# The first half-step's down projection as seven block products, with their differences and weight sums on Pool

## What is computed

```python
def swiglu(h, wg, wu, wd):
    return (jax.nn.silu(h @ wg) * (h @ wu)) @ wd

def ffn_half(x, g, wg, wu, wd):
    return x + 0.5 * swiglu(rms_norm(x, g), wg, wu, wd)
...
        x = ffn_half(x, g_ffn1[l], w1_gate[l], w1_up[l], w1_down[l])
        u = rms_norm(x, g_mix[l])
        qkv, z, qm, gates = split_proj(u, w_in[l])
```

## Time and profile before

| | |
|---|---|
| median of three timed runs | 2451.17 us |
| profiled execution, span from first to last instruction | 2449.4 us |
| gate and up stage of the first half-step, PE's first matmul to its last | 35.7 to about 506 us |
| down projection, PE's first matmul to its last | 506.5 to 755.1 us |
| busy PE, DVE, ACT, Pool over the span | 97%, 58%, 38%, 25% |

### The profile page before, as it was taken

One profiled execution on the slowest core, in us unless ns is written; L12 is line 12 of the kernel. 1 busy time (PEld: TensorE's weight loads), 2 busy tenths in 40 slices (PEclk: granted clock), 3 DMA queues, 4 the chain that ended last, 5 costly groups with the idle time before them and its releaser, 6 DMA issues.

```text
span 2449.4 us, 41688 instructions
## 1 busy us (share of the span) xinstructions
PE 2371.0 (97%) x16883; PEld 2321.8 (95%) x16883; DVE 1420.3 (58%) x2364; ACT 920.4 (38%) x1906; POOL 614.8 (25%) x614
## 2 busy tenths in 40 slices
PE   5899999999999999999899999999699999999998
PEld 4899999999998899999899999999699999999998
DVE  7766666645565274544364644468866566654546
ACT  5433343334453132333332222145433333333544
POOL 1544444501120020000200200014445444431100
PEclk7999999999999999999999999999999999999999
DMA  3122222265553461122342633124122222255645
GB/s 108 53 79 79 78 79 87 70 208 183 185 186 117 157 209 42 58 64 63 84 141 81 188 98 130 44 78 129 57 83 79 79 78 79 79 173 170 201 161 176
DMA packets 176934, 275.10 MB, mean 112 GB/s; under 512 B 11461, under 2 KB 124613, under 8 KB 176360
## 3 DMA queue, kind: packets, MB, share of 16 engines
q1 hardware_dynamic: 159848, 208.75, 26.3%
q0 software_dynamic: 16896, 63.70, 7.9%
HBM read 227.57 MB, written 44.84 MB: 111 GB/s over the span
## 4 chain that ended last, share of the span: by engine, by line
PE 46%; DVE 2%; ACT 1%; issue 1%; DMA 0%; POOL 0%; SPq 0%; DVEq 0%; ACTq 0%
PE ps L426 9%; PE ps L427 9%; PE ps L428 9%; PE ps L1162 6%; PE ps L1163 6%; PE ps L1164 6%; DMA blend_late_l<-mem_out 0%; PE ps L2889 0%; PE ps L927 0%; DVE ul_full L533 0%; DVE ul L2685 0%; DVE ul L529 0%; DVE blend_rights L529 0%; ACT uh L525 0%; DVE ffn_tok L960 0%
## 5 line engine op out<-in xcount | busy, mean ns | idle before, releaser
L426 PE MATMUL ps<-uh,stream_high 128*128 128x352 f32 (+1 forms) x1392 | 457.7, 329 | 8.6 <-DVEq L2727 7.0
L427 PE MATMUL ps<-uh,stream_low 128*128 128x352 f32 (+1 forms) x1392 | 446.5, 321 | 0.0
L428 PE MATMUL ps<-ul,stream_high 128*128 128x352 f32 (+1 forms) x1392 | 444.7, 319 | 0.0
L426 PEld LDWEIGHTS ps<-uh,stream_high 128*128 128x128 f32 x1392 | 262.8, 189 | 19.7 <-issue 16.9
L1277 DVE TENSOR_TENSOR ffn_part<-ffn_part,ps 128x258 f32<-128x258 f32 x352 | 147.1, 418 | 210.9 <-PE ps L1164 148.9
L427 PEld LDWEIGHTS ps<-uh,stream_low 128*128 128x128 f32 x1392 | 262.8, 189 | 1.6 <-issue 1.0
L428 PEld LDWEIGHTS ps<-ul,stream_high 128*128 128x128 f32 x1392 | 262.8, 189 | 0.0
L1196 ACT ACTIVATE ffn_part<-ps 128x258 f32<-128x258 f32 x264 | 102.0, 386 | 423.3 <-PE ps L1164 415.4
L1162 PE MATMUL ps<-uh,ffn_lefts_h 128*128 128x258 f32 x704 | 199.1, 283 | 6.3 <-ACT ffn_part L1196 3.4
L1162 PE MATMUL ps<-uh,stream_high 128*128 128x258 f32 x704 | 199.6, 284 | 3.2 <-ACT ffn_part L1196 3.2
L1163 PE MATMUL ps<-uh,ffn_lefts_l 128*128 128x258 f32 x704 | 199.0, 283 | 0.0
(11 more groups left out here) (374 smaller groups left out, 6273.6 us busy)
## 6 DMA issues: line engine op xcount, KB each, us to landing
ffn_raw_d<-in_w_down SPq DMA_DIRECT2D x66, 512.0 KB, 3.3
stream_raw<-in_w_in SPq DMA_DIRECT2D x25, 1024.0 KB, 5.5
ffn_hid_out<-ffn_hid SPq DMA_DIRECT2D x88, 258.0 KB, 2.4
stream_raw<-in_w_gate SPq DMA_DIRECT2D x22, 1024.0 KB, 5.3
stream_raw<-in_w_up SPq DMA_DIRECT2D x22, 1024.0 KB, 5.6
stream_raw<-in_w_down SPq DMA_DIRECT2D x88, 256.0 KB, 3.1
stream_raw<-in_w_out SPq DMA_DIRECT2D x22, 512.0 KB, 3.9
ffn_raw_d<-in_w_down SPq DMA_DIRECT2D x44, 256.0 KB, 3.1
```

The costliest lines, as they stand in the source:

```text
L426: pe.matmul(out, w_high, a_high, start=first, stop=False)
L427: pe.matmul(out, w_low, a_high, start=False, stop=False)
L428: return pe.matmul(out, w_high, a_low, start=False, stop=last)
```

## The change

The down projection's product is cut into two by two blocks on each side: output halves of 512 channels, hidden tiles by pairs (the even and the odd tile of a pair), and columns in two blocks (n = 0, 1) of twice 258. Seven products of such blocks, each over all 11 pairs, replace the eight.

- **Operands.** `Pieces` prepares them during the gate and up stage. For each pair Pool makes the four weight sums (`Pieces.gpsimd`) and, for each j, the four differences of hidden blocks in three instructions (`differ`), and SP stores rows, differences and sums to memory. They are formed in the space of `x`, which is stored once after the first side and comes back in four pieces (`load_x`).
- **Rounds.** `Rounds` runs the products one after another in the order of `ROUNDS`, 7 rounds of 11 steps. A step loads 128x512 of weights or sums and 2x258 columns into a ring of six, where the raw data and the low part share their space; the load of step s therefore waits until step s - 6 is done. Each step is 2 x 4 banks x 3 matmuls of 258 columns. `OPENS` names the rounds that clear the banks; the others go on accumulating. Behind the split of step 3 of a round DVE adds the previous round's banks onto one block of `x` (`INTO`).
- **Seam.** The last four steps run first for j = 0 and then for j = 1. Squares and split parts are made in rounds 4 to 6 and during those last steps; what concerns the last quarter (`LATE`) is done in the next stage, whose third unit now begins with four mean matmuls and whose DVE list begins with four reciprocals of 258 columns.

The diff, cut to its core:

```diff
-class Down:
...
+ROUNDS = (5, 3, 2, 1, 6, 7, 4)
+OPENS = (5, 2, 1)
+INTO = {5: (1, 1), 3: (0, 1), 2: (0, 0), 1: (0, 0), 6: (0, 1), 7: (1, 1), 4: (1, 0)}
...
+    def load(self, sp, p, rights):
+        if p == 0:
+            sp.wait_ge(self.x_stored, 16)
+            sp.wait_ge(rights.gained, 4)
+            sp.wait_ge(rights.gained_act, 4 * K2)
+        else:
+            sp.wait_ge(self.summed, 4 * p)
+        sp.dma_start(self.raw, self.w[:, 2 * p:2 * p + 2, :]).then_inc(self.down_in, 16)
...
+    def store_sums(self, sp, p):
+        sp.wait_ge(self.summed, 4 * (p + 1))
+        sp.dma_start(self.cols[:, :, p, :], self.sums).then_inc(self.sums_stored, 16)
...
+    def gpsimd(self, gp, p):
+        low, high = (slice(half * WIDE, (half + 1) * WIDE) for half in range(2))
+        gp.wait_ge(self.down_in, 16 * (p + 1))
+        if p:
+            gp.wait_ge(self.sums_stored, 16 * p)
+        gp.tensor_tensor(self.sums[:, 0, :], self.raw[:, 0, high], self.raw[:, 1, high], ALU.add).then_inc(self.summed, 1)
+        gp.tensor_tensor(self.sums[:, 2, :], self.raw[:, 0, low], self.raw[:, 0, high], ALU.subtract
+                         ).then_inc(self.summed, 1)
+        gp.wait_ge(self.summed, 4 * p + 1)
+        gp.tensor_tensor(self.sums[:, 1, :], self.sums[:, 0, :], self.raw[:, 0, low], ALU.subtract
+                         ).then_inc(self.summed, 1)
+        gp.wait_ge(self.summed, 4 * p + 3)
+        gp.tensor_tensor(self.sums[:, 3, :], self.raw[:, 1, low], self.sums[:, 1, :], ALU.subtract
+                         ).then_inc(self.summed, 1)
...
+    def differ(self, gp, p, j, hid, hid_ready, rights):
+
+        at = 3 * (2 * p + j)
+        d = self.diffs
+        gp.wait_ge(*hid_ready)
+        if p == 0:
+            gp.wait_ge(self.x_stored, 16)
+            gp.wait_ge(rights.gained, 4)
+            gp.wait_ge(rights.gained_act, 4 * K2)
+        else:
+            gp.wait_ge(self.diffs_stored[j], 16 * p)
+        gp.tensor_tensor(d[:, j, 0:2, :], hid[:, j, 1:4:2, :], hid[:, j, 0:2, :], ALU.subtract).then_inc(self.differed, 1)
+        gp.wait_ge(self.differed, at + 1)
+        gp.tensor_tensor(d[:, j, 2, :], hid[:, j, 3, :], d[:, j, 0, :], ALU.subtract).then_inc(self.differed, 1)
+        gp.wait_ge(self.differed, at + 2)
+        gp.tensor_tensor(d[:, j, 3, :], hid[:, j, 2, :], d[:, j, 2, :], ALU.subtract).then_inc(self.differed, 1)
...
+    RING = 6
+    STEPS = len(ROUNDS) * PAIRS
+    GROUPS = 2 * HO
+    APART = 4
+    LEAD = 4
+    PIECE_AT = 5
+    X_AT = (None, 14, 20, 44)
...
+    def load(self, sp, s):
+        r, p = divmod(s, PAIRS)
+        product_of, slot, pieces = ROUNDS[r], s % self.RING, self.pieces
+        if s >= self.RING:
+            self.wait_step(sp, s - self.RING)
+        if product_of in DIRECT:
+            tile, half = DIRECT[product_of]
+            src = pieces.w[:, 2 * p + tile, half * WIDE:(half + 1) * WIDE]
+        else:
+            sp.wait_ge(pieces.sums_stored, 16 * (p + 1))
+            src = pieces.cols[:, SUM_SLOT[product_of], p, :]
+        sp.dma_start(self.left_raw[:, slot, :], src).then_inc(self.left_in[slot], 16)
+        for stored in pieces.rows_stored if ROW_SLOT[product_of] < 4 else pieces.diffs_stored:
+            sp.wait_ge(stored, 16 * (p + 1))
+        sp.dma_start(self.right_raw[:, slot, :, :], pieces.rows[:, ROW_SLOT[product_of], p, :, :]
+                     ).then_inc(self.right_in[slot], 16)
...
+        half, block = self.X_ORDER[n]
+        for j in range(2):
+            at = slice(half * HO, (half + 1) * HO)
+            sp.dma_start(self.m.x[:, at, columns(block, j)], self.pieces.x_out[:, at, columns(block, j)]
+                         ).then_inc(self.x_back[n], 16)
+
+    def sync(self, sp):
+        for s in range(self.RING, self.STEPS):
+            if s in self.X_AT:
+                self.load_x(sp, self.X_AT.index(s))
+            self.load(sp, s)
...
+    def tensor(self, pe, s, js, taken):
+        r, p = divmod(s, PAIRS)
+        slot, opens = s % self.RING, ROUNDS[r] in OPENS
+        pe.wait_ge(self.ready, s + 1)
+        for j in js:
+            for i in range(HO):
+                b = HO * j + i
+                if p == 0 and r == 0 and i == 0:
+                    pe.wait_ge(taken, TAKES * (2 * SIDES - 1 + j))
+                if p == 0 and r:
+                    pe.wait_ge(self.added, self.GROUPS * (r - 1) + b + 1)
...
+                pe.matmul(out, w_h, a_h, start=opens and p == 0, stop=False, skip_group_check=True)
+                pe.matmul(out, w_l, a_h, start=False, stop=False, skip_group_check=True)
+                last = pe.matmul(out, w_h, a_l, start=False, stop=p == PAIRS - 1, skip_group_check=True)
+                if p == PAIRS - 1:
+                    last.then_inc(self.done, 1)
+        if p < PAIRS - 1 and len(js) == 2:
+            last.then_inc(self.step_done, 1)
...
+        for s in range(together):
+            self.tensor(pe, s, (0, 1), taken)
+        for j in range(2):
+            for s in range(together, self.STEPS):
+                self.tensor(pe, s, (j,), taken)
...
+        slot, count = s % self.RING, 16 * (s // self.RING + 1)
+        act.wait_ge(self.left_in[slot], count)
+        act.activation(self.left_h[:, slot, :], self.left_raw[:, slot, :], ACT.Copy).then_inc(self.rounded, 1)
+        act.wait_ge(self.right_in[slot], count)
+        act.activation(self.right_h[:, slot, :, :], self.right_raw[:, slot, :, :], ACT.Copy).then_inc(self.rounded, 1)
...
+    def add(self, dve, r, j, i):
+        half, block = INTO[ROUNDS[r]]
+        b = HO * j + i
+        if b == 0:
+            dve.wait_ge(self.x_back[self.X_ORDER.index((half, block))], 32)
+        dve.wait_ge(self.done, self.GROUPS * r + b + 1)
+        x = self.x_piece(half * HO + i, block, j)
+        dve.scalar_tensor_tensor(x, self.m.ps[:, b, 0:QW], 0.5, x, ALU.mult, ALU.add).then_inc(self.added, 1)
...
+    def tensor(self, pe, c):
+
+        u, self.unit = self.unit, self.unit + 1
+        before = len(self.WHOLE + self.FIRST)
+        if u == 0:
+            pe.wait_ge(self.low, before)
+        if u == 1:
+            pe.wait_ge(self.low, before + HO)
+        if u == 2:
+            pe.wait_ge(self.summed, before - 2)
...
+                pe.matmul(self.m.ps[:, self.BANKS[b], 0:QW], self.m.mean[:, :], self.m.rstd[:, columns(n, j)],
+                          start=True, stop=True).then_inc(self.meaned, 1)
+        if u == 3:
+            pe.wait_ge(self.rooted, 4)
...
+    def vector(self, dve):
+        for i, (o, n, js) in enumerate(self.LATE):
+            self.low_of(dve, len(self.WHOLE + self.FIRST) + i + 1, o, n, js)
+        dve.wait_ge(self.summed, len(self.WHOLE + self.FIRST) - 2)
...
+            late = self.m.rstd[:, columns(0, 1)]
+            dve.tensor_tensor(late, late, self.late_sq[:, i, :], ALU.add).then_inc(self.late_summed, 1)
...
                     lefts.load(sp, q + 1)
+                    if pieces and q == 0:
+                        pieces.store_x(sp)
+                    if pieces and q and q % 2 == 0:
+                        pieces.store_diffs(sp, q // 2 - 1, 1)
+                        pieces.store_sums(sp, q // 2 - 1)
+                    if pieces and q % 2:
+                        pieces.load(sp, q // 2, rights)
                 elif then is not None:
                     sp.wait_ge(lefts.ready, ALL * SIDES)
                     stream.load(sp, stream.base, *then)
                 if finish and q == SIDES - 1:
                     finish.sync_first(sp, (lefts.ready, ALL * SIDES))
+                if pieces and q == SIDES - 1:
+                    pieces.load(sp, q // 2, rights)
                 if q % 2:
                     store(q // 2, 0)
+                    if pieces:
+                        pieces.store_diffs(sp, q // 2, 0)
                     if q == SIDES - 1:
                         if finish:
                             finish.sync_second(sp, (product_done, done(q, 0, ALL - 1)))
                         else:
                             sp.wait_ge(product_done, done(q, 0, ALL - 1))
-                            for s in range(DOWN_RING):
+                            for s in range(down.RING):
                                 down.load(sp, s)
                     store(q // 2, 1)
             if finish:
                 finish.sync(sp)
                 return
-            for s in range(DOWN_RING, DOWN_STEPS):
-                down.load(sp, s)
+            pieces.store_sums(sp, PAIRS - 1)
+            pieces.store_diffs(sp, PAIRS - 1, 1)
+            down.load_x(sp, 0)
+            down.sync(sp)
 
         @block.tensor
         def _(pe):
...
+            for s in range(3, down.STEPS):
+                r, p = divmod(s, PAIRS)
                 down.vector(dve, s)
...
+                if r and p == down.LEAD - 1:
+                    for j in range(2):
+                        for i in range(HO):
+                            down.add(dve, r - 1, j, i)
```

(74 more changed lines are left out.)

241 lines of the change are left out of this document (155 added, 86 removed).

## The result

The changed kernel took 2463.45 us (median of 4 runs, 2461.56 to 2464.86) against 2451.18; the ratio is 1.0048, 95% interval 1.0034 to 1.0062. The forecast was 2433.5, its range 2421 to 2447. In a later series of nine runs the same kernel took 2458.17, ratio 1.0025 [1.0016, 1.0035].

A forecast was written before the change was run, and what follows sets the result against it. TensorE's matmuls were taken to bound both the gate and up stage and the down projection. Terms: -27.6 + 0.5 + 4.2 + 3.1 + 2.6 - 0.5 = -17.7 us, from 2451.17 to 2433.5 us; range 2421 to 2447.

The forecast's parts named there:

- Pool in the gate and up stage: Gate and up stage: Pool's added sums and differences fit where it waits; cost 0.5 us for the whole stage, from 0 to 10.
- The fourth rival: Gate and up stage: VectorE and Pool hold each other up, 0.5 us in each of 20 sides; 2443, chance 0.08.
- The rival on the slower side: Gate and up stage: Pool becomes the bound, 44 us a pair against 40.2, 42 us more, 2475; chance 0.08.
- Matmuls: Down projection: 1848 matmuls of 258 columns take 221.0 us against 248.6 before, -27.6 us.
- Step 6: Down projection, first round: TensorE waits 4.2 us, from 0 to 8, for a load queued behind stores and the first x piece.
- First round start: Down projection: TensorE waits 0.2 us for the first add, plus 1.9 for x queued before a load: 2.1 us.
- other round start: Down projection: TensorE waits 0.2 us for the first add at each; all six round starts together 3.1 us, from 0 to 15.
- the clock: Down projection: TensorE runs at half speed after the waits of 4.2 and 2.1 us, costing 2.6 us, from 0 to 5.
- Seam: Down projection's end to the front stage's fourth unit: 19.2 us instead of 19.7, -0.5, from -2 to +4.

## Why the prediction was wrong

- **Pool in the gate and up stage: the step that failed.** "I take 0.5 us for the whole stage, from 0 to 10"; it was 30.1 (23.5 to 26 in the later series). The sizes were right: Pool about 32 us per pair, the split's price beside Pool. The argument was not: "the odd sides become like them", the even ones. In the even sides of the kernel before Pool leaves gaps: in one (277.78 to 287.04) the seven splits take 9.3 us from the first to the last, 0.80 each on average, with Pool busy for 5.6 us beside them. In the odd side they ran almost alone and took 9.0 (257.00 to 266.01). With Pool busy for 12.9 us beside them they take 13.9 (269.00 to 282.87), 1.33 each, and the raw buffer, the up load, Pool's sums and ScalarE's split are each later with it. I had covered lateness of Pool's sums by 5 us of slack, without asking what releases the load that they wait for. The slack of that chain is about 3 us by the runs, an estimate: with the sums moved the splits take 1.9 us and the up load 1.1 us longer than before, and TensorE is idle for only 2 of 370 us; in the changed kernel it is 4.9 and 1.0, and a pair loses 2.9. Leaving the sums out took back all but 0.7 us; moving them all but some 4, ahead of the new wait at its end (518.63 less 8.54 is 510.1).
- **The fourth rival** named the mechanism at 0.5 us a side, with a chance of 0.08; it was 1.5 a side, so its 2443 was too low as well. The rival on the slower side (Pool as the bound) did not come: Pool had 92 us idle in 370, and the time did not follow its work in the run with the sums moved.
- **Matmuls**: 221.0 forecast; the stage takes 229.5 with its waits and, with x fetched later, 223.2 less the 2.1 of the stage change, 221.1. Right.
- **Step 6**: 4.2 forecast, 2.25 at 556.34. **First round start**: 2.1 forecast, 4.04 at 574.98. No other round start waits 0.1 us, where 0.2 each was forecast. With the clock it is 8.4, forecast 9.9.
- **Seam**: 19.2 forecast, 20.5 from the last matmul's end (766.04) to 786.52, with the forecast wait for a reciprocal at the fourth unit; after the pause eleven matmuls of the first unit followed at 0.29 us instead of 0.16 (granted clock 0.50 from 769.70 to 773.00, the lower of its two levels, 1.2 GHz), 1.4 us where 0.8 was charged. The forecast had added its parts wrongly: two units, four means, root, reciprocals and the take come to 17.2, not 16.3, and the seam to 20.1.
- Together, from the first down matmul to the fourth front unit: -18.2 forecast, -18.4 measured. That it fits so closely is luck: the waits and the clock came out 1.5 us lower, the seam 1.3 higher.

## What to carry to other kernels

Idle time of an engine is no free place if another engine reads beside it: look up which of that engine's instructions get longer, and follow what their last one releases (a buffer, its load, what waits for the load) round to the next use. Move such work to where the other engine idles before giving up on it: here the same instructions made the next stage start 23 to 30 us late in one place and about 4 in another, apart from a wait in the queue that could be removed. After moving a store, see what it now stands ahead of in its queue at the end of the loop.

## What was not expected of the hardware

The same gate and up stage ended up to 6.6 us apart in different series (start of the down projection 530.0 to 536.6), where the medians of the kernel before lie within 0.9 us (2451.18, 2451.64, 2452.03). That a full TensorE hides what a chain through several engines and the queue passes on would explain it; in the first series the up load took 7.0 us (median of ten), in the three other runs of this stage 6.7, which over ten pairs is 3 of the 4 to 6.6 us. Why it took longer there stays open. And 1.5 MB of stores beside a 1 MB load made it land in 7.0 instead of 6.0 us (median of ten up loads), which cost nothing as soon as the splits ended in time.
